# Five experts in place of four loaded ahead of the routing, with 64 places each, and the four large places sorted among the other eleven

## The chip, the cores and the metric

The kernel runs on one core of one Trainium2 chip, as one launch. The metric is the time on the device in microseconds (us), the median of the runs. Engines are named PE (TensorE), DVE (VectorE), ACT (ScalarE), POOL (GpSimd) and SP (SyncE, which issues nearly all loads of weights).

## What is computed

A trunk of four layers on 384 tokens (128 of context, 256 latents) of width 1024. Each layer is a token mixer followed by a mixture of 16 experts, of which each token takes two. Cut to the part that matters here:

```python
def moe(h, w_router, router_bias, w_gate, w_up, w_down):
    s = jax.nn.sigmoid((h @ w_router).astype(jnp.float32))
    ...
    _, idx = lax.top_k(jnp.where(emask, sb, -jnp.inf), TOP_K)      # TOP_K = 2, one group of four experts
    ...
    a = jnp.einsum('bsd,edf->bsef', h, w_gate)       # 16 experts, 1024 x 256 each
    u = jnp.einsum('bsd,edf->bsef', h, w_up)         # 1024 x 256
    act = jax.nn.silu(a) * u * gates[..., None].astype(h.dtype)
    return jnp.einsum('bsef,efd->bsd', act, w_down)  # 256 x 1024
```

With float32 weights each of an expert's three matrices is 1 MB, so a layer's experts are 48 loads of 1 MB.

## The kernel before

**Places.** The kernel computes an expert only for the tokens that chose it. 384 tokens with two experts each are 768 rows; they are sorted into 1152 places. Four experts, the first `FIXED = 4`, have 64 places each whatever the router says. The other 12 are sorted by load in each layer: the four with the most rows get 96 places, the other eight 64. Which expert stands at which of these 12 positions is known only on the chip, when the router has run; its number is written into the small array `held`. In what follows expert e means position e in this order, and Ge, Ue and De are the loads of its gate, up and down matrices.

**Blocks.** The 1152 places are 9 blocks of 128, each of four tiles of 32 rows. A block is computed on PE by a gate-up of 64 matmuls (32 rows against 512 columns each), 8 transposes, and the down projection of 32 matmuls, which is issued one block late: gate-up(b), transposes, down(b−1), gate-up(b+1). A tile belongs to one expert, and before the change the experts of the blocks' tiles are

```
block 0: 0 0 1 1    block 3: 5 5 6 6    block 6: 10 10 11 11
block 1: 2 2 3 3    block 4: 6 7 7 7    block 7: 12 12 13 13
block 2: 4 4 4 5    block 5: 8 8 9 9    block 8: 14 14 15 15
```

More rows than places for an expert go to further steps of their own, which are run only if there are such rows.

**Weights.** SP issues the loads one after the other into 15 slots of 1 MB: 0 to 7 are the `ring`, 8 and 9 lie in `V`, 10 to 12 in `work`, 13 and 14 in `gbc`. A load waits on the semaphore `slot_used` of its slot, which the last user of the slot's earlier contents increments, and SP issues nothing past a load that waits. The order of the loads and the slot of each are planned when the kernel is built, by `plan_ring`: it has an estimated begin and end for the use of each load, takes among the next 16 the one that can start soonest, and charges 2.45 us for a load or 2.9 us for one of an expert from `FIXED` on. `homes` says which slots a load may go to, `opens` from when.

Loads of the experts below `FIXED` have a fixed address and can be issued during the mixer. A load of another expert reads its number from `held` (L763), after SP has waited once per layer for `held_ready` (the sort is done) and for `near_issued` (POOL has issued the gathers of the tokens' rows).

Of the kernel before, what the change touches and what calls it, by code (L numbers as in the profile page):

```python
# [25 lines left out]
UC = 256  # L26
R = 8
TILE = 32
FIXED = 4
WIDE, NARROW = 3 * TILE, 2 * TILE  # L30
LARGE = 4
SIZES = [NARROW] * FIXED + [WIDE] * LARGE + [NARROW] * (E - FIXED - LARGE)
STARTS = [sum(SIZES[:i]) for i in range(E)]
# [106 lines left out]
def last_block(i):  # L140

    return (STARTS[i] + SIZES[i] - 1) // P
# [65 lines left out]
def phase_of(key):  # L208

    name, L = key[0], key[1]  # L210
    if name[:3] == "moe":
        return L, "moe"
    return (L - 1, "route") if name == "mod" and key[2] < 2 and L > 0 else (L, "main")


def homes(key):

    name, (L, phase) = key[0], phase_of(key)
    if name in ("moe_g", "moe_u"):
        pairs = ((0, 1), (2, 3), (8, 9), (10, 11)) + (((4, 5),) if key[2] >= FIXED else ())  # L220
        return [pair if name == "moe_g" else pair[1:] for pair in pairs]
    if name == "moe_d":
        late = (13,) if last_block(key[2]) < BLOCKS - 3 else tuple(range(6)) + (8, 9, 10, 11) if key[2] >= E - FIXED else ()
        return [(slot,) for slot in (6, 7, 12) + late]
    if name == "wo":
        return [(slot,) for slot in (4, 5, 6, 7)]
    if phase == "route":
        return [(2,), (3,), (12,)] if key[2] == 0 and key[3] < 3 else [(slot,) for slot in (4, 5, 6, 7, 13)]
    if name == "ukv":
        return [(slot,) for slot in (0, 1, 2, 3)]  # L230
    if name == "mod" and key[2] < 2:
        return [(slot,) for slot in range(R)]
    return [(slot,) for slot in tuple(range(R)) + ((9, 13, 14) if KINDS[L] < 2 else (13, 14))]
# [15 lines left out]
def plan_ring():  # L249
# [5 lines left out]
    def opens(key):  # L255
        name, phase = key[0], phase_of(key)
        if name[:3] == "moe" and key[2] >= FIXED:
            return mark["held", phase[0]]
        return 0.0

    def choice(key):
        if key[0] == "moe_u":
            return None
        phase = phase_of(key)
        free = {home: max(max(free_at[s], home_opens(s, phase, mark)) for s in home) for home in homes(key)}
        best = min(free, key=free.get)
        at = max(free[best], opens(key))
        safe = [k for k in waiting if k != key and not (key[0] == "moe_g" and k == ("moe_u",) + key[1:])]
        return (at, best) if not safe or at <= min(begin[k] for k in safe) else None
# [8 lines left out]
    while waiting:  # L278
# [5 lines left out]
        at, _, key, home = min(found)  # L284
        span = LOAD_SPAN_MOE if key[0][:3] == "moe" and key[2] >= FIXED else LOAD_SPAN
        now = at + span * len(home)
# [53 lines left out]
def build(nc, A):  # L340
# [4 lines left out]
    with ctx:  # L345
        def sb(name, shape):
            return ctx.enter_context(nc.sbuf_tensor(name, shape, F32))
# [47 lines left out]
        move_of = sb("move_of", [P, E])  # L395
        place_key = sb("place_key", [P, E - FIXED])
        place_of = sb("place_of", [P, E - FIXED])
# [2000 lines left out]
```

## Time and profile before

| | |
|---|---|
| median of 3 runs | 1530.26 us (1529.27 to 1533.38) |
| the profiled execution, its time and its span | 1539.47 us, 1537.7 us |
| PE busy | 1399.2 us, 91% of the span |
| DVE, ACT, POOL busy | 624.9, 346.7, 233.2 us |
| SP's DMA queue (q1) | 95686 packets, 346.13 MB, 59.6% of the 16 DMA engines' time |
| all DMA | 412.96 MB, mean 269 GB/s |

The rows of the profile have start and length in us. `issue` in a chain is time in which the engine waited for nothing that the profile shows by name; PE's waits for the landing of weights are among it. All matmuls of the experts are issued by one helper, so that they have one line, L1867, and they are told apart by their number (64 for a gate-up, 32 for a down, 96 where both follow without a break) and by their place in the stage. The four expert stages lie at about 265 to 376, 606 to 730, 1025 to 1147 and 1389 to 1510 us.

### The profile page before, as it was taken

How to read it: one execution, taken by the hardware profiler on the slowest of the kernel's cores; microseconds unless marked ns; L12 is line 12 of the kernel's file. 1: busy time of each engine (PE TensorE's matmuls, PEld its weight loads, DVE VectorE, ACT ScalarE, POOL GpSimd, SP SyncE). 2: the span in 40 equal slices, each digit the busy share in tenths (PEclk: the TensorE clock that was granted, in tenths of full speed). 3: DMA queues.
4: the chain of work that ended last, by engine and by line, in shares of the span. 5: the costliest groups of instructions: out<-in, count | busy, mean ns of one | idle time of the engine just before them, and what ended most of it. 6: DMA issues, size and time to landing. Idle time of an engine off the chain costs nothing.

```text
span 1537.7 us, 25812 instructions
## 1 busy us (share of the span) xinstructions
PE 1399.2 (91%) x10352; PEld 844.3 (55%) x10352; DVE 624.9 (41%) x1450; ACT 346.7 (23%) x933; POOL 233.2 (15%) x295
## 2 busy tenths in 40 slices
PE   4999998998998998898989999988989999969985
PEld 1876685332776686333664456853327766854332
DVE  0136625433456525242522343254334247252435
ACT  1105512110214612110210343121102036121101
POOL 0100022111122022110200000221112000212103
PEclk9999999999999999999989999999999999979998
DMA  9998138999978238999857502489999880238994
GB/s 332 331 313 278 73 107 325 386 420 414 331 284 238 83 131 295 386 416 420 321 212 248 118 29 96 162 328 381 420 414 340 286 307 2 82 124 299 421 422 166
DMA packets 121633, 412.96 MB, mean 269 GB/s; under 512 B 13531, under 2 KB 55486, under 8 KB 96934
## 3 DMA queue, kind: packets, MB, share of 16 engines
q1 hardware_dynamic: 95686, 346.13, 59.6%
q0 software_dynamic: 18880, 61.23, 12.2%
q10 hardware_dynamic: 6944, 3.91, 0.8%
q8 instruction: 85, 1.39, 0.4%
q14 instruction: 38, 0.31, 0.1%
HBM read 387.12 MB, written 26.66 MB: 269 GB/s over the span
## 4 chain that ended last, share of the span: by engine, by line
PE 73%; DMA 8%; DVE 8%; issue 4%; ACT 3%; POOL 1%; SPq 1%; DVEq 0%; POOLq 0%; ACTq 0%
PE bank L1867 65%; PE bank L2037 3%; ACT pp L1165 2%; PE bank L2202 2%; DMA y_slots<-kT 2%; DMA V<-in_swa_wqkv 1%; DMA ids<-own_id,row_of 1%; DVE x L1297 1%; DMA hT<-h_rows,id_of 1%; PE bank L1922 1%; DMA xn<-y_slots,row_of 1%; DMA id_of<-ids 1%; DVE hT L1289 1%; SPq L689 1%; PE bank L2214 1%
## 5 line engine op out<-in xcount | busy, mean ns | idle before, releaser
L1867 PE MATMUL bank<-ring,pp 128*32 128x512 f32 x2112 | 342.9, 606 | 17.4 <-issue 13.4
L1867 PE MATMUL bank<-ring,hT 128*128 128x256 f32 (+3 forms) x998 | 233.3, 392 | 5.3 <-DVE hT L1289 2.7
L1867 PEld LDWEIGHTS bank<-ring,hT 128*128 128x128 f32 x998 | 181.3, 191 | 54.2 <-issue 26.8
L1867 PE MATMUL bank<-work,pp 128*32 128x512 f32 x704 | 176.1, 609 | 8.6 <-DVE kT L1735 5.1
L1867 PEld LDWEIGHTS bank<-ring,pp 128*32 128x32 f32 x2112 | 92.5, 111 | 157.5 <-issue 155.7
L1867 PE MATMUL bank<-ring,xn 128*128 128x256 f32 x768 | 168.2, 380 | 0.0
L1867 PEld LDWEIGHTS bank<-ring,xn 128*128 128x128 f32 x768 | 145.0, 190 | 19.4
L1867 PE MATMUL bank<-V,pp 128*32 128x512 f32 x480 | 114.0, 629 | 5.3 <-issue 4.7
L1165 ACT ACTIVATE pp<-bank,neg_max 128x384 f32<-128x384 f32 x192 | 96.7, 525 | 13.3 <-DVE neg_max L1631 10.1
L1743 DVE TENSOR_TENSOR pp<-bank,pp 128x256 f32<-128x256 f32 x36 | 15.3, 425 | 198.0 <-ACT pp L1235 198.0
L910 POOL TENSOR_TENSOR x<-x,pp 128x256 f32<-128x256 f32 x48 | 38.3, 799 | 371.0 <-DVE pp L1704 371.0
L1735 DVE TENSOR_TENSOR kT<-bank,xn 128x512 f32<-128x512 f32 x72 | 46.4, 687 | 113.6 <-PE bank L1867 107.6
L1867 PE MATMUL bank<-ring,condT 128*32 128x256 f32 x1120 | 77.6, 418 | 8.5 <-DMA ring<-in_w_mod 8.5
L1867 PE MATMUL bank<-kT,work 64*128 64x384 f32 (+3 forms) x384 | 81.1, 456 | 4.7 <-ACT work L1153 2.5
L1631 DVE TENSOR_REDUCE neg_max<-bank 128x1 f32<-128x384 f32 x192 | 79.0, 460 | 14.2 <-PE bank L1867 14.2
L1867 PEld LDWEIGHTS bank<-work,pp 128*32 128x32 f32 x704 | 44.2, 112 | 67.6 <-issue 67.1
L2037 PE MATMUL bank<-ident,pp 128*128 128x128 f32 x448 | 70.7, 284 | 11.6 <-ACT pp L1165 7.5
L1704 DVE TENSOR_TENSOR pp<-bank,gbc 128x256 f32<-128x256 f32 x48 | 20.4, 425 | 137.8 <-PE bank L1867 137.8
L1278 DVE COPY work<-bank 128x256 f32<-128x256 f32 (+1 forms) x27 | 13.9, 514 | 143.5 <-PE bank L1867 143.5
L1235 ACT ACTIVATE pp<-bank 128x256 f32<-128x256 f32 x36 | 13.8, 385 | 243.6 <-PE bank L1867 243.6
L2037 PEld LDWEIGHTS bank<-ident,pp 128*128 128x128 f32 x448 | 48.1, 142 | 36.9 <-ACT pp L1165 17.4
L1867 PEld LDWEIGHTS bank<-ring,condT 128*32 128x32 f32 x1120 | 36.9, 119 | 44.4 <-DMA ring<-in_w_mod 13.4
(279 smaller groups left out, 1793.3 us busy)
## 6 DMA issues: line engine op xcount, KB each, us to landing
ring<-in_w_mod SPq DMA_DIRECT2D x70, 1024.0 KB, 8.2
ring<-in_moe_w_gate SPq DMA_DIRECT2D x40, 1024.0 KB
ring<-in_moe_w_up SPq DMA_DIRECT2D x40, 1024.0 KB, 15.6
ring<-in_moe_w_down SPq DMA_DIRECT2D x36, 1024.0 KB
gbc<-in_w_mod SPq DMA_DIRECT2D x17, 1024.0 KB, 11.8
work<-in_moe_w_down SPq DMA_DIRECT2D x16, 1024.0 KB, 15.2
y_slots<-kT POOLq DMA_DIRECT2D x28, 512.0 KB, 8.6
work<-in_moe_w_gate SPq DMA_DIRECT2D x12, 1024.0 KB
```

The costliest lines, as they stand in the source:

```text
L689: sp.dma_start(dst.rearrange("p (k n) -> p k n", k=shape), src).then_inc(slot_full[slot], 16)
L910: nc.gpsimd.tensor_tensor(xs, xs, wo_tmp[:, g % 4, :], ALU.add).then_inc(x_mixed, 1)
L1165: ins = nc.scalar.activation(pp[:, 0, odd, at:at + w], job_bank(("S", L, j, half, odd))[:, c0:c0 + w], ACT.Exp, bias=neg_max[:, h, b:b + 1 ...
L1289: ins = V_.tensor_scalar(hT[:, k, b * P:(b + 1) * P], job_bank(key)[:, k * P:(k + 1) * P], amul[:, s, k, c:c + 1], modc[:, 2 * s, k, c:c + ...
L1297: link(V_.scalar_tensor_tensor(out=x[:, b, :], in0=rows[b], scalar=wk_early[:, k, b:b + 1], in1=x[:, b, :], op0=ALU.mult, op1=ALU.add))
L1631: last = V_.tensor_reduce(neg_max[:, h, b:b + 1], job_bank(key)[:, c0:c0 + w], AX.X, ALU.max, negate=True)
L1704: V_.tensor_tensor(wo_tmp[:, g % 4, :], job_bank(key)[:, 0:UC], gbc[:, 0, COND[b], u * UC:(u + 1) * UC], ALU.mult).then_inc(wo_mul, 1)
L1735: V_.tensor_tensor(ys[:, blk % 2, cols], bank[4 + half][:, :], slot_gate[:, cols], ALU.mult).then_inc(evacuated, 1)
L1867: return pe.matmul(out, lhsT, rhs, start=start, stop=stop)
L1922: ins = pe.transpose(job_bank(key)[:, k * P:(k + 1) * P], scaled[n % 2][b][:, at:at + P], ident[:, :])
L2037: ins = pe.transpose(bank[4 + odd][:, t * P:(t + 1) * P], pp[:, 0, odd, 512 * half + t * P:512 * half + (t + 1) * P], ident[:, :])
L2202: ins = pe.transpose(bank[6 + k // 4][:, k % 4 * P:(k % 4 + 1) * P], xg[:, slot, k * P:(k + 1) * P], ident[:, :])
```

## The change

`FIXED` becomes 5, so that five experts have fixed numbers and 64 places, and the four large places are sorted among the other eleven. The number of places, 1152, and of blocks, 9, stays.

```diff
@@ -26,7 +26,7 @@
-FIXED = 4
+FIXED = 5
 WIDE, NARROW = 3 * TILE, 2 * TILE
 LARGE = 4
 SIZES = [NARROW] * FIXED + [WIDE] * LARGE + [NARROW] * (E - FIXED - LARGE)
@@ -217,7 +217,7 @@
     name, (L, phase) = key[0], phase_of(key)
     if name in ("moe_g", "moe_u"):
-        pairs = ((0, 1), (2, 3), (8, 9), (10, 11)) + (((4, 5),) if key[2] >= FIXED else ())
+        pairs = ((0, 1), (2, 3), (8, 9), (10, 11)) + (((4, 5),) if key[2] >= FIXED - 1 else ())
```

What hangs on `FIXED`: the experts of blocks 2 to 4 become 4 4 5 5, 5 6 6 6 and 7 7 7 8 (the other blocks stay); `held` and the arrays of the sort have 11 entries in place of 12; G4, U4 and D4 have a fixed address and no wait for `held_ready`; and `plan_ring` gives another order and other slots. The second line lets G4 and U4 still use slots 4 and 5.

The order on SP, early in the first layer's expert stage (G is `in_moe_w_gate`, U is `in_moe_w_up`, D is `in_moe_w_down`; this piece begins with D0). Before:

```order
L689 DMA work<-in_moe_w_down 128x2048 [waits slot_used12,states,o_ready]
L689 DMA ring<-in_moe_w_down 128x2048 [waits slot_used6]
L689 DMA ring<-in_moe_w_down 128x2048 [waits slot_used7]
L689 DMA gbc<-in_moe_w_down 128x2048 [waits slot_used13,wo_mul]
L763 TENSOR_LOAD held [waits near_issued,held_ready]
L763 ISA x2
L689 ISA [waits slot_used4]
L689 DMA ring<-in_moe_w_gate 128x2048
L689 DMA ring<-in_moe_w_up 128x2048 [waits slot_used5]
```

After, at the same place:

```order
L689 DMA work<-in_moe_w_down 128x2048 [waits slot_used12,states,o_ready]
L689 DMA ring<-in_moe_w_down 128x2048 [waits slot_used6]
L689 DMA ring<-in_moe_w_gate 128x2048 [waits slot_used4]
L689 DMA ring<-in_moe_w_up 128x2048 [waits slot_used5]
L689 DMA ring<-in_moe_w_down 128x2048 [waits slot_used7]
L689 DMA gbc<-in_moe_w_down 128x2048 [waits slot_used13,wo_mul]
L763 TENSOR_LOAD held [waits near_issued,held_ready]
L763 ISA x2
L689 ISA [waits slot_used0]
L689 DMA ring<-in_moe_w_gate 128x2048
```

G4 and U4 have moved ahead of D2, D3 and the wait for `held_ready`; the first load behind the wait is G5, into slot 0. (In the fourth layer they stand between D2 and D3.)

The second place is the end of the same stage on SP. Before, the piece goes from D10 to D12:

```order
L689 DMA ring<-in_moe_w_down 128x2048 [waits slot_used7]
L763 TENSOR_LOAD held
L763 ISA x2
L689 ISA [waits slot_used4]
L689 DMA ring<-in_moe_w_gate 128x2048
L689 DMA ring<-in_moe_w_up 128x2048 [waits slot_used5]
L689 DMA ring<-in_moe_w_down 128x2048 [waits slot_used6]
L763 TENSOR_LOAD held
L763 ISA x2
L689 ISA [waits slot_used0]
L689 DMA ring<-in_moe_w_gate 128x2048
L689 DMA ring<-in_moe_w_up 128x2048 [waits slot_used1]
```

After, from D10 to U15:

```order
L689 DMA work<-in_moe_w_down 128x2048 [waits slot_used12]
L689 DMA ring<-in_moe_w_down 128x2048 [waits slot_used4]
L763 TENSOR_LOAD held
L763 ISA x2
L689 ISA [waits slot_used0]
L689 DMA ring<-in_moe_w_gate 128x2048
L689 DMA ring<-in_moe_w_up 128x2048 [waits slot_used1]
L763 TENSOR_LOAD held
L763 ISA x2
L689 ISA [waits slot_used10]
L689 DMA work<-in_moe_w_gate 128x2048
L689 DMA work<-in_moe_w_up 128x2048 [waits slot_used11]
```

The order was D10, G14, U14, D11, G15, U15, and is D10, D11, G14, U14, G15, U15. In all layers the loads ahead of U15 are the same ones. The order of the instructions of PE, ACT, POOL and DVE does not move; DVE's operations of the sort are 11 and 121 elements wide in place of 12 and 144.

## Rows read from the trace of the kernel before

**Rows 1.** The page: busy us, share of the span, instructions of PE and others

```profile
PE 1399.2 (91%) x10352; PEld 844.3 (55%) x10352; DVE 624.9 (41%) x1450; ACT 346.7 (23%) x933; POOL 233.2 (15%) x295
```

**Rows 2.** Windows: stretch, us, busy PE to POOL, granted clock, DMA share, GB/s

```profile
602.00:611.40 9.40, 7.69 (x70) 7.45 (x66) 7.29 (x32) 0.96 (x2) 3.03 (x3) 1.00 1.03 350
628.00:702.00 74.00, 70.72 (x611) 24.87 (x607) 27.46 (x45) 8.83 (x20) 12.52 (x13) 0.98 1.01 414
...
284.00:374.00 90.00, 83.13 (x725) 29.45 (x728) 33.65 (x54) 9.59 (x22) 12.34 (x13) 0.98 1.02 420
...
1044.00:1144.00 100.00, 92.10 (x789) 31.91 (x785) 34.67 (x56) 10.56 (x24) 13.57 (x15) 0.97 1.00 413
...
1361.00:1387.80 26.80, 16.16 (x105) 15.25 (x106) 17.54 (x82) 4.29 (x8) 3.99 (x5) 0.62 0.16 60
1397.00:1402.00 5.00, 2.91 (x20) 1.26 (x22) 3.04 (x6) 2.52 (x4) 0.24 (x1) 0.81 0.90 54
```

**Rows 3.** Timeline of SP's loads: start, us; second layer, then fourth layer

```profile
602.21 0.33 SPq L689 DMA_DIRECT2D gbc<-in_moe_w_down  x1
611.39 0.17 SPq L689 DMA_DIRECT2D ring<-in_moe_w_gate  x1
...
702.42 0.37 SPq L689 DMA_DIRECT2D ring<-in_moe_w_up  x1
...
1356.15 0.33 SPq L689 DMA_DIRECT2D gbc<-in_moe_w_down  x1
1387.87 0.17 SPq L689 DMA_DIRECT2D ring<-in_moe_w_gate  x1
...
1396.93 0.33 SPq L689 DMA_DIRECT2D ring<-in_moe_w_gate  x1
...
1409.65 0.34 SPq L689 DMA_DIRECT2D V<-in_moe_w_gate  x1
```

**Rows 4.** The chain late in the four stages: start, us, what

```profile
346.88 2.60 issue
349.49 8.41 PE bank L1867 x64
...
358.93 1.47 issue
360.39 3.67 PE bank L1867 x32
...
701.74 7.07 PE bank L1867 x64
...
709.84 3.12 issue
712.96 5.37 PE bank L1867 x32
...
1127.21 2.80 issue
...
1475.67 2.76 issue
1478.43 8.77 PE bank L1867 x64
...
1494.54 10.54 PE bank L1867 x96
```

**Rows 5.** PE's timeline where gate-up(8) starts, in the first three layers

```profile
365.57 8.79 PE L1867 MATMUL bank<-ring,pp 128*32 128x512 f32 x80 [1.10 <-issue]
...
718.66 10.51 PE L1867 MATMUL bank<-ring,pp 128*32 128x512 f32 x96
...
1135.71 10.51 PE L1867 MATMUL bank<-ring,pp 128*32 128x512 f32 x96
```

**Rows 6.** DMA issues from 702.0 to 704.5 us: KB, us to landing

```profile
ring<-in_moe_w_up SPq DMA_DIRECT2D x1, 1024.0 KB, 15.4
```

**Rows 7.** Window of gate-up(7) in the first layer, columns as in rows 2

```profile
349.40:358.90 9.50, 9.41 (x72) 3.28 (x72) 1.09 (x4) 0.39 (x1) 0.00 (x0) 0.85 1.01 423
```

## The prediction

> **What bounds the kernel now.** I began with the busy times: PE works 1399.2 us of the 1537.7 us span [rows 1], so only its waits can give anything, and a later view has to say what ends them in the expert stages. The windows by stretch come second. In the second layer's stage (L1) the DMA engines are busy all the time: a share of 1.03 from 602.0 to 611.4 us, 1.01 from 628 to 702 us at 414 GB/s [rows 2]. A load is 1,048,576 bytes, so it costs 1.048576/414 = 2.53 us of that stream. The first and the third layer look the same, 1.02 and 1.00 over 90 and 100 us [rows 2]. The reader is to see here that the stream of weights has no hole in those three layers. The fourth (L3) has one: a share of 0.16 from 1361 to 1387.8 us [rows 2].
>
> Third comes SP's timeline, which tells when loads are issued. In L1 SP issues D3 (into `gbc`) at 602.21 and then nothing until G4 at 611.39 [rows 3], because it waits for `held_ready` and `near_issued`. Over just those 9.2 us the DMA share is 1.03 [rows 2]: the queue is still emptying what stands in it. SP's pause costs no byte. In L3, D3 goes out at 1356.15 and G4 at 1387.87 [rows 3], and there the share of 0.16 shows the queue empty.
>
> Fourth, the chain of waits, with the names of the blocks put to it by counting (a block is a gate-up of 64 matmuls, 8 transposes, then the down projection of the block before, 32 matmuls). PE waits late in each stage. L1: gate-up(7) takes 7.07 us from 701.74; at 709.84 PE waits 3.12 us for D11, then down(6) takes 5.37 us; gate-up(8) follows at 718.66 [rows 4, 5]. L0: 2.60 us before gate-up(7), 1.47 before down(6). L2: 2.80 before down(6). L3: 2.76 before gate-up(7) [rows 4].
>
> **What pins gate-up(8).** U15, the last load that it needs, is issued at 702.42 in L1 and lands 15.4 us later [rows 3, 6]: 717.82 us, and gate-up(8) starts at 718.66. So block 8 starts when U15 has landed, whatever PE did before.
>
> **The change, part by part.**
>
> *Early move, L0 to L2: 0 us.* G4 and U4 no longer read the register of a held expert, so they go ahead of D2 and D3 and of SP's wait. In a queue without a hole that only swaps places: 2.53 × 2 = 5.1 us earlier for two loads, 5.1 us later for D2 and D3, and U15 behind the same number of bytes. The first load behind the wait is now G5, and D3 leaves the queue two loads later, so the queue is if anything fuller there. D2 and D3 are first used by down(1), some 20 us on, so their delay costs nothing; without that cover it would cost up to 5.1 us in each layer. If the queue did run dry, the gain could reach those 5.1 us; the share of 1.03 excludes it.
>
> *Early move, L3: −1.4 us.* Here G4 and U4 really fill a hole. But G5 waits for slot 0, which block 0's gate-up gives back, and is issued at 1396.93 now [rows 3] and still is. From 1397 to 1402 the queue hardly moves, 54 GB/s [rows 2], so the four loads G5, U5, G6, U6 end at about 1402 + 4 × 2.53 = 1412.1 us. G7 waits for block 1's slot and is issued at 1409.65 [rows 3]. The stream can't get ahead of that: the gain lies between 0 and 1412.1 − 1409.65 = 2.5 us. An issued load needs some time before its bytes move; I take 1.4, about the middle.
>
> *Late move: D11 ahead of G14 and U14, into slot 4.* D11 now lands two loads (5.1 us) earlier. It was waited for 1.47 to 3.12 us, so the wait before down(6) goes in all four layers. U15 has the same loads ahead of it, so its landing stays. Its slots (10 and 11 in place of 0 and 1) must be free in time: the landing lag of 15.4 us is six loads of queue, and a slot given back some us later would still find bytes ahead. What PE gains before down(6) it therefore waits before gate-up(8). Worked out:
> - L0: gate-up(7) and its transposes end at 358.93, down(6) takes 3.57 without a fall of the clock, the turns 0.5: ready at 363.0. Gate-up(8) starts at 365.57 [rows 4, 5]. New wait 2.6, start as before.
> - L1: 709.84 + 4.1 = 713.9, landing 717.8: wait 3.9 to 4.2. The start moves from 718.66 to about 718.15 (down(6) with its slow clock had ended a little after the landing): −0.5.
> - L2: 1127.21 + 4.1 = 1131.3 against a start at 1135.71 [rows 4, 5]: wait 3.9, also −0.5.
> - L3: the wait of 2.76 shrinks to 1.4 and gate-up(7) then takes 7.07 in place of 8.77 [rows 4]; ready at 1475.67 + 1.4 + 7.07 + 1.02 + 4.0 = 1489.2; the landing moves from before 1494.54 to before 1493.1: wait 3.9, −1.4.
>
> *The clock after the new wait.* After 2.60 us without work gate-up(7) took 8.41 us in place of 7.07, after 2.76 it took 8.77; after 3.12 down(6) took 5.37 in place of about 3.6; after 1.47 down(6) took 3.67 [rows 4]. The granted clock of gate-up(7) in L0 is 0.85 on average [rows 7], so part of it ran at 1.2 GHz in place of 2.4. A long wait thus costs 1.3 to 1.8 us more. In L1 and L2 that price is paid now on down(6), where it lies in front of U15's landing and costs nearly nothing. In the changed kernel it falls on gate-up(8), and behind that nothing waits for a load that is late anyway: it is on the path. I take +1.3 for L0 (the same 2.60 us), +1.75 each for L1 and L2, +1.7 for L3. Bounds: 0 each, and 1.8 each.
>
> The Trainium skill, page "TensorE: Matmul & The Clock Gate", section "HAM oscillation — how this bites in real kernels", describes a kernel whose waits for DMA between short stretches of matmuls send the clock down each time. This case's trace agrees, with 8.77 for 7.07 us after a 2.76 us wait; by the page as by the rows the longer wait before block 8 speaks against the change.
>
> *Everything else: 0.* DVE's sorting operations get 11 wide where they were 12; they take about 0.3 us each and are fixed cost mostly. One register fewer is read per layer while the queue is deep. Expert 8's weights are needed one block earlier (block 4 holds a part of it); the order gives them some 4 us of slack in L0, my count of places in the queue, and more elsewhere. With that slack gone, each layer would lose what is missing. The work of PE is the same 9 blocks.
>
> **Sum.** L0 +1.3; L1 −0.5 + 1.75 = +1.25; L2 +1.25; L3 −1.4 + 1.7 = +0.3. Together +4.1, of which I let some 0.4 go for what a narrower sort and a better filled queue may give: +3.7. The profiled execution took 1539.47 us with its span of 1537.7, so 1543.2 for such a one; the median of the runs shown is 1530.26, 9.2 below, and the difference is carried over: **1534.0 us**.
>
> **The rivals.**
> 1. *The two early loads are a gain in every layer.* SP's pause ends sooner for PE: 5.1 us in each of four layers, 1530.3 − 20 = 1510 us. For it speaks only the pause of 9.2 us in SP's timeline; against it the share of 1.03 in it. Chance 0.05. The Trainium skill, page "DMA: Bandwidth & Descriptors", section "Rules for kernel authors", says to issue a load early and to wait for it late; by that rule this is what the change would do. The trace speaks against it in three layers of four.
> 2. *No fall of the clock is added and L3 gains more,* by gathers that run while the queue is empty: −2.4 without the clock's price, and another −2.5 to −4 in L3: about 1525 us. Chance 0.07.
> 3. *Slower: the merged wait costs its full price.* Place: gate-up(8) of all layers. 4 × 1.8 − 1.0, and no gain in L3 because the stall at 1397 to 1402 swallows it: +6.2, 1536.5 us. It decides once the price is over 1.9 us a layer, or L3's gain stays away. For it: the new waits (3.9 us) are longer than any in the rows. Chance 0.24. If the low clock lasted twice as long as it does after 2.8 us, it were 4 × 3.5 − 2.4 = +11.6, 1542 us. Chance 0.06.
> 4. *Expert 4 gets more than 64 rows* where it had 96, and the overflow steps run: 3 passes × 16 experts with 3 loads of 2.53 us each is 364 us more for one such layer, about 1895 us. Before there were none and I count at most 59 rows for expert 4 in these inputs. Chance 0.02.
> 5. *The forecast,* merged waits with part of their price given back: 0.56.
>
> **How the numbers follow.** A measurement of this kernel can tell about 0.3%, 4.6 us, from no change. Same is the forecast's 0.56. Faster is 0.05 + 0.07 = 0.12; slower 0.24 + 0.06 + 0.02 = 0.32. The range goes from no price at all (−2.4, 1527.9) and a bit of case 2 up to case 3 with its run-to-run share of 2 us: 1527 to 1539. Outside it are case 1, most of case 2, the doubled fall and the overflow, 0.2 in all.
>
> **What would show it.** Right: D11 no longer waited for in any layer; one wait of 2.6 to 4.2 us before gate-up(8), starting within 0.5 us of today's place (L3: 1.4 earlier) as counted from the stage's start; gate-up(8) at 8.4 to 8.8 us; the DMA share still at 1.00 from the router to D15 in L0 to L2. Wrong: U15's landing earlier by two loads in L0 to L2 (case 1); U15 late because its slots 10 and 11 come free late; a wait before gate-up(4) or down(4) for expert 8; gate-up(8) at 7.07 us.

## The result

The changed kernel takes 1541.24 us (median of 20 runs, 1533.13 to 1550.74), the kernel before, run beside it, 1534.16 us (20 runs, 1529.02 to 1540.01). The ratio is 1.0046, interval 1.003 to 1.0062: slower by 7.1 us of 1534. The forecast was 3.7 us slower, "same" the likeliest and "slower" at 0.32. The direction was right. The time of 1541.24 lies outside the range of 1527 to 1539. Of the 7.2 us between the forecast of 1534.0 and this time, 3.9 come from its base: it started from the 1530.26 of three runs, and twenty runs of the same kernel give 1534.16. The other 3.4 were missing in the sum. One run of warm (5014.88 us) and one of late_alone (1845.43 us), two of the experiments below, were slow and stand in no ratio.

The two profiled executions, 1539.47 us before and 1541.63 after, lie only 2.2 us apart. That hides 4.6 us: between the third and the fourth expert stage the profiled execution of before took 237.9 us (end of down(8) at 1151.57 to gate-up(0) at 1389.47), that of after 233.3 us (1155.56 to 1388.81), and those of the nine executions of the experiments below 233.1 to 235.8. So the stages are compared by themselves, from the start of gate-up(0) to the end of down(8):

| us, from PE's timeline | L0 | L1 | L2 | L3 | sum |
|---|---|---|---|---|---|
| stage, before | 121.40 | 122.75 | 122.80 | 120.91 | 487.86 |
| stage, after | 121.41 | 125.49 | 123.98 | 123.84 | 494.72 |
| start of gate-up(8), after − before | +0.01 | +0.10 | −1.59 | −1.76 | −3.24 |
| from there to the start of down(8), before | 12.21 | 12.21 | 12.22 | 12.20 | |
| the same, after | 12.21 | 14.85 | 14.99 | 15.19 | +8.40 |
| down(8), after − before | 0 | 0 | 0 | +1.70 | +1.70 |

The stages are 6.9 us longer, close to the measured 7.1. The closeness is partly luck, for these are single executions: two of one and the same kernel (late_undone, below) differ by 4.0 us in this sum. The stretch from gate-up(8) to down(8) is steadier: in the four executions with D11 behind U14 it takes 12.20 to 12.29 us in all 16 layers. In these two profiles all of the loss lies behind the start of gate-up(8).

### The profile page after: what moved, and what is told of

The parts are those of the page before. It is cut to its first block, busy times and chain, and to the rows that moved or that the text cites. A ratio compares the mean times of both kernels' runs of the same rounds, so it can differ in the third digit from the quotient of the medians.

```text
span 1539.8 us, 25784 instructions
## 1 busy us (share of the span) xinstructions
PE 1396.0 (91%) x10352; PEld 842.3 (55%) x10352; DVE 624.5 (41%) x1450; ACT 346.7 (23%) x933; POOL 233.6 (15%) x295
## 3 DMA queue, kind: packets, MB, share of 16 engines
q0 software_dynamic: 18880, 61.07, 12.2%
## 4 chain that ended last, share of the span: by engine, by line
PE 70%; DMA 11%; DVE 7%; issue 5%; ACT 3%; POOL 2%; SPq 1%; another core or an unknown queue 0%; POOLq 0%; DVEq 0%; ACTq 0%
PE bank L1867 62%; PE bank L2037 3%; ACT pp L1165 2%; DMA hT<-h_rows,id_of 2%; PE bank L2202 1%; DMA V<-in_swa_wqkv 1%; DMA ids<-own_id,row_of 1%; DMA id_of<-ids 1%; DMA ring<-in_moe_w_gate 1%; DMA work<-in_moe_w_gate 1%; DMA y_slots<-kT 1%; PE bank L1922 1%; DMA xn<-y_slots,row_of 1%; POOL ids L924 1%; SPq L689 1%
## 5 line engine op out<-in xcount | busy, mean ns | idle before, releaser
L1867 PE MATMUL bank<-ring,pp 128*32 128x512 f32 x2064 | 375.0, 608 | 31.3 <-issue 19.2
L1867 PEld LDWEIGHTS bank<-ring,pp 128*32 128x32 f32 x2064 | 99.7, 112 | 190.0 <-issue 188.1
L1867 PE MATMUL bank<-V,pp 128*32 128x512 f32 x496 | 117.2, 627 | 2.7 <-issue 2.2
## 6 DMA issues: line engine op xcount, KB each, us to landing
ring<-in_moe_w_gate SPq DMA_DIRECT2D x37, 1024.0 KB, 12.5
gbc<-in_w_mod SPq DMA_DIRECT2D x17, 1024.0 KB, 11.6
```

What stands on the lines that cost most here:

```text
L1867: return pe.matmul(out, lhsT, rhs, start=start, stop=stop)
```

## The profile after

The page of the changed kernel, busy times and the queue that SP feeds:

```profile
PE 1396.0 (91%) x10352; PEld 842.3 (55%) x10352; DVE 624.5 (41%) x1450; ACT 346.7 (23%) x933; POOL 233.6 (15%) x295
q1 hardware_dynamic: 95686, 346.13, 59.4%
```

PE does the same 10352 instructions as in [rows 1] and the queue carries the same bytes. Busy times tell nothing here. SP's timeline in L1 (start, us, what), first the early place, then the tail:

```profile
595.21 0.33 SPq L689 DMA_DIRECT2D work<-in_moe_w_down  x1
596.06 0.33 SPq L689 DMA_DIRECT2D ring<-in_moe_w_down  x1
598.88 0.33 SPq L689 DMA_DIRECT2D ring<-in_moe_w_gate  x1
600.61 0.33 SPq L689 DMA_DIRECT2D ring<-in_moe_w_up  x1
600.98 0.47 SPq L689 DMA_DIRECT2D ring<-in_moe_w_down  x1
601.56 0.47 SPq L689 DMA_DIRECT2D gbc<-in_moe_w_down  x1
618.47 0.35 SPq L689 DMA_DIRECT2D ring<-in_moe_w_gate  x1
...
684.64 0.38 SPq L689 DMA_DIRECT2D ring<-in_moe_w_down  x1
695.46 0.34 SPq L689 DMA_DIRECT2D ring<-in_moe_w_gate  x1
```

G4 went out at 598.88, 12.5 us earlier than in [rows 3], and SP then issued nothing for 16.9 us (601.56 to 618.47), since G5 waits for block 0's slot. The windows (columns as in [rows 2]) say that the queue was never dry in these stretches of L1, and that in L3 it was:

```profile
601.60:618.40 16.80, 14.88 (x132) 10.00 (x133) 7.07 (x31) 0.92 (x2) 7.72 (x8) 1.00 1.02 374
628.00:702.00 74.00, 68.35 (x591) 24.04 (x587) 28.37 (x46) 8.84 (x20) 12.69 (x14) 0.98 1.01 417
1361.00:1396.00 35.00, 22.81 (x178) 17.14 (x177) 18.57 (x84) 4.87 (x9) 10.11 (x11) 0.76 0.31 110
```

A pause of SP nearly twice as long as before's still costs no byte: the share is 1.02 within it. Now the chain at the end of the stage in L1 (start, us, what), which answers to the rows from 701.74 of [rows 4]:

```profile
715.23 2.83 issue
718.06 13.19 PE bank L1867 x96
```

The wait of 3.12 us ahead of down(6) is gone, and one of 4.01 us is ahead of gate-up(8), where PE's timeline shows it (the number in brackets is the idle time), beside a wait of 1.53 us ahead of gate-up(7) that cost nothing:

```profile
701.94 0.62 PE L1867 MATMUL bank<-ring,pp 128*32 128x512 f32 x2 [1.53 <-issue]
...
718.06 1.07 PE L1867 MATMUL bank<-ring,pp 128*32 128x512 f32 x2 [4.01 <-issue]
```

A pair of matmuls takes 0.62 us behind the wait of 1.53, and 1.07 behind the wait of 4.01. The windows of two us show why, in the last but two column, the granted clock:

```profile
709.00:714.00 5.00, 5.00 (x44) 2.05 (x42) 1.20 (x3) 0.97 (x2) 0.00 (x0) 1.00 1.04 428
714.00:716.00 2.00, 0.04 (x1) 0.00 (x0) 1.89 (x3) 0.37 (x1) 0.29 (x1) 1.00 0.96 397
716.00:718.00 2.00, 0.00 (x0) 0.00 (x0) 1.32 (x2) 0.00 (x0) 0.24 (x1) 0.65 1.01 422
718.00:720.00 2.00, 1.94 (x12) 0.68 (x16) 0.00 (x0) 0.00 (x0) 0.00 (x0) 0.50 1.01 420
720.00:722.00 2.00, 2.00 (x12) 0.45 (x8) 0.00 (x0) 0.00 (x0) 0.00 (x0) 0.50 1.00 420
722.00:724.00 2.00, 2.00 (x16) 0.59 (x12) 0.00 (x0) 0.00 (x0) 0.00 (x0) 0.64 1.02 426
724.00:726.00 2.00, 2.00 (x24) 0.67 (x20) 0.00 (x0) 0.00 (x0) 1.17 (x2) 1.00 1.04 434
```

The clock falls to 0.50, which is 1.2 in place of 2.4 GHz, within the wait and is still there in 718 to 722 us and for most of 722 to 724 (0.64), with 12 matmul records in two us where there are 24 at full clock. By these windows that is some 5.4 us of gate-up(8) at half clock (an estimate), which makes the 2.64 us that it takes longer. In L3 the chain has the fall twice:

```profile
1489.34 2.79 issue
1492.12 8.43 PE bank L1867 x64
...
1505.87 1.30 DVE kT L1735 x2
1507.17 0.14 issue
1507.31 5.37 PE bank L1867 x32
```

Gate-up(8) takes 8.43 for 7.07 us, and down(8), which is short of work before it, 5.37 for about 3.6. Here the rows of matmuls alone would mislead: the 96 matmuls from 1492.12 read 11.83 us, but DVE's next step comes only at 1505.87, 13.75 us after their start. That is why the table counts from start to start. ACT's next step is late too, 1.83 us behind the start of the last transposes (0.54 in the kernel before, L1), though the granted clock reads 1.00 (two windows, then two rows of the timeline):

```profile
1496.00:1498.00 2.00, 2.00 (x24) 0.67 (x20) 0.00 (x0) 0.00 (x0) 0.00 (x0) 1.00 0.98 404
1504.00:1506.00 2.00, 0.39 (x2) 0.20 (x2) 0.13 (x1) 0.29 (x1) 0.82 (x1) 1.00 0.82 287
...
1503.88 0.51 PE L2214 MATMUL bank<-ident,pp 128*128 128x128 f32 x2
1505.71 0.37 ACT L669 COPY pp<-bank 128x256 f32<-128x256 f32 x1 [4.41 <-PE bank L2214]
```

Both engines wait for PE here. So of the 8.40 us in the table, 5.4 are gate-up(8)'s own matmuls (9.71, 8.50 and 8.39 us in L1 to L3 for 7.07). The other 3.0 come in L2 and L3 behind them, where PE waits 2.62 and 2.92 us ahead of down(8) in place of 1.27, at a granted clock of 1.00. That PE really finished later than its records say is the likely reading; what held it up is not shown.

In L0 the wait ahead of gate-up(7) was 2.64 us, gate-up(7) took 10.03 us in place of 8.41, and PE came late enough to gate-up(8) that only 1.02 us of wait was left, with no fall (10.51 us). There the clock's price was paid ahead of U15's landing, and L0 lost nothing.

## The experiments

All ratios are to the kernel before, timed beside each. "Stages" is the sum of the four stages as in the table, of the profiled execution, against 487.86 before. "Block 8" is what the four stretches from the start of gate-up(8) to down(8) take over 4 × 12.2 us. The code pieces are shortened to the lines that matter.

| | ratio (interval) | stages | block 8 |
|---|---|---|---|
| the change | 1.0046 (1.003 to 1.0062) | +6.9 | 8.4 |
| old_plan | 0.9982 (0.9964 to 1.0001) | −0.2 | 0 |
| new_plan | 1.0144 (1.0123 to 1.0165) | +24.3 | 6.4 |
| late_undone | 0.9981 (0.9961 to 1.0001) | +0.9 | 0.1 |
| late_undone_2 | 0.9989 (0.9972 to 1.0006) | +4.9 | 0 |
| early_undone | 1.003 (1.0013 to 1.0048) | +7.0 | 4.5 |
| late_alone | 1.0049 (1.0024 to 1.0073) | +9.2 | 10.7 |
| warm | 1.0064 (1.0044 to 1.0084) | +10.4 | 0.9 |
| warm_short | 1.0009 (0.9991 to 1.0027) | +3.7 | 1.4 |
| warm_half | 1.003 (1.001 to 1.0049) | +10.4 | 4.4 |

**1. old_plan: the change without its order of loads**

```diff
-    ring_place, ring_order = plan_ring()
+    ring_place, ring_order = planned(4)     # plan_ring() under FIXED = 4 and the STARTS that go with it
```

> The changed kernel in all (five fixed experts, places, sort of eleven), but its loads in the order and slots of the kernel before: D2, D3, then G4, U4 and D11 behind U14. My theory, that the cost sits in D11 ahead of G14 and U14 and the one long wait that it makes before gate-up(8): a ratio to the kernel before of 1.000 (0.998 to 1.002), gate-up(8) with down(7) at 10.5 us in L1 to L3. Rival, that the new mix of experts in the blocks or the narrower sort costs it: 1.004 to 1.005, as the changed kernel.

Measured: 0.9982, waits of before's kind (in L1 2.04 us ahead of gate-up(7), 1.14 ahead of down(6), 1.11 ahead of gate-up(8)), and 12.2 us from gate-up(8) to down(8) in all four layers. So 64 places for expert 4, the new mix of experts in blocks 2 to 4 and the sort of eleven cost nothing. The order of loads does. One part of the early move stays in this run: G4 and U4 stand behind D3, but have no wait for `held_ready`, and in L1 G4 goes out at 601.72 us, where it was 611.39.

**2. new_plan: the order and slots of the change on the kernel before**

```diff
+    ring_place, ring_order = planned(5)
+    for L in range(DEPTH):        # G4 and U4 stay behind D3
+        ring_order = behind(ring_order, [("moe_g", L, 4), ("moe_u", L, 4)], ("moe_d", L, 3))
```

> The kernel before in all (four fixed experts), but its loads in the order and slots of the changed one, only G4 and U4 kept behind D3 and the wait for held_ready. My theory: a ratio of 1.004 to 1.006, a wait of about 4 us before gate-up(8) in L1 to L3 and 12 to 13 us for gate-up(8) with down(7). Rival, that the early move or the places cost it: 1.000.

Measured: 1.0144, more than any theory gave. The timeline of SP and a window in its L1 show what I had overlooked:

```profile
677.07 0.34 SPq L689 DMA_DIRECT2D work<-in_moe_w_gate  x1
677.51 0.38 SPq L689 DMA_DIRECT2D work<-in_moe_w_up  x1
693.94 0.33 SPq L689 DMA_DIRECT2D ring<-in_moe_w_down  x1
...
690.00:702.00 12.00, 12.00 (x109) 4.05 (x108) 4.34 (x6) 1.41 (x5) 2.23 (x2) 1.00 0.73 259
```

The changed plan puts G11 into slot 10 behind G6 and, next after U11, D9 into slot 7 behind D6. In the changed kernel expert 6 ends in block 3, in the kernel before in block 4, one block of 12 us later. So D9 goes out 16.4 us after U11 (677.51 to 693.94), where it is 9.0 us in the changed kernel (666.43 to 675.38). SP issues in order, so all loads behind D9 wait too; the queue falls behind (share 0.73 from 690 to 702 us) and gate-up(7) waits 7.14 us. This run tests the late move only together with this hole, so it is no evidence for my theory. It shows that a plan belongs to its places.

**3. late_undone: the change with D11 back behind U14**

```diff
     for L in range(DEPTH):
+        order = behind(order, [("moe_d", L, 11)], ("moe_u", L, 14))
```

> The changed kernel with one pair swapped back in each layer: D11 issued behind U14, slots as in the changed kernel, G4 and U4 early. My theory: the wait splits again into one before down(6) and none or a short one before gate-up(8), the fall of the clock lies in front of U15's landing, ratio to the kernel before 0.998 to 1.001. Rival, that slots 10, 11 or the early move are to blame: 1.004 to 1.005.

Measured: 0.9981. The chain in L1:

```profile
711.85 3.26 issue
715.11 3.67 PE bank L1867 x32
```

PE's timeline has 1.11 us idle ahead of gate-up(8), and 12.20 us from its start to down(8), in L1 as in the other layers. One position in the order, that of D11, makes the whole difference between 1.0046 and 0.998: about 0.6%, 9 to 10 us by the two runs of this kernel, against 8.4 + 1.7 in the table of stages. The changed plan also moves D8 ahead of G10 and U10 and gives other slots, which the section on the change leaves out; late_undone keeps both, so they are not what costs.

**4. early_undone: the change with only its early move undone**

```diff
+        order = behind(order, [("moe_g", L, 4), ("moe_u", L, 4)], ("moe_d", L, 3))
...
-                if (L, FIXED) not in held_at and e >= FIXED:
+                if (L, FIXED) not in held_at and e >= FIXED - 1:
```

(the second edit stands ahead of the direct load, so that G4 waits for `held_ready` as before)

> The changed kernel with only its early move undone: G4 and U4 issued behind D3 and behind the wait for held_ready and near_issued, the tail (D11 ahead of G14 and U14) as in the changed kernel. My theory, that the early move gives nothing in L0 to L2 and 1.4 to 1.8 us in L3: a ratio to the kernel before of 1.004 to 1.007, U15 at its place in L0 to L2 and some 1.5 us later in L3. Rival, that G4 and U4 ahead of D2 and D3 do harm (to the gathers, or by D2 and D3 late): 1.000 to 1.002.

Measured: 1.003, below the expected 1.004 to 1.007 and above the rival's 1.000 to 1.002. From gate-up(8) to down(8) it took 14.44 us in L1 and L3, behind waits of 3.99 and 2.44 us, and 12.20 in L0 and L2. In L0 the wait was 2.28 us, without a fall; in L2 a slow gate-up(7) of 9.97 us had left only 1.09 us of it. In L3 gate-up(8) starts 104.77 us into the stage, 103.31 in the change and 105.07 before. The ratios (1.003 and 1.0046) overlap. The cost remains without the early move.

**5. late_alone: the kernel before with only the late move**

```diff
+        new.update({("moe_d", L, 11): 4, ("moe_g", L, 14): 0, ("moe_u", L, 14): 1, ("moe_g", L, 15): 2,
+                    ("moe_u", L, 15): 3, ("moe_d", L, 12): 5, ("moe_d", L, 13): 6})
+        order = behind(order, [("moe_d", L, 11)], ("moe_d", L, 10))
```

> The kernel before with only the late move: D11 issued right behind D10 and ahead of G14 and U14. So that it needs no slot that comes free late, D11 goes to slot 4, G14 and U14 to 0 and 1, G15 and U15 to 2 and 3, D12 and D13 to 5 and 6. My theory: a ratio of 1.004 to 1.007, one wait of about 4 us before gate-up(8) and 12 to 13.2 us for gate-up(8) with down(7) in most layers. Rival, that the late move costs only together with the new places or the early loads: 0.999 to 1.001.

Measured: 1.0049. Its chain in L1:

```profile
717.70 2.78 issue
720.49 13.61 PE bank L1867 x96
...
735.76 1.45 PE bank L1867 x9
```

The waits ahead of gate-up(8) are 4.00, 4.32, 4.33 and 2.31 us in L0 to L3, and from its start to down(8) it takes 15.30, 15.27, 14.89 and 14.04 us against 12.2. This is what new_plan was meant to be: the late move alone, on the kernel before, with slots that come free in time, costs as much as the change.

**6. warm, warm_short, warm_half: the order of the change, with work for PE in the wait**

```diff
+                    pe.wait_ge(act_full, n + 1)
+                    for _ in range(WARM.get((L, blk), 0)):
+                        mm(bank[slot][:, 0:P], ident[:, :], ident[:, :], True, True)
                     for e in sorted(set(of)):
                         wait_unit(("moe_g", L, e))
```

> The changed kernel, order of loads untouched, with added matmuls of ident by ident on PE (128 columns each, about 0.13 us by the transposes' rate) into the bank that gate-up(8) overwrites, before it waits for its weights: 28 ahead of gate-up(8) in each layer, 14 ahead of gate-up(7) in L0 and L3. My theory, that the price is the low clock after the wait: gate-up(8) with down(7) at 10.5 us in all layers, starting where it starts now; L3's 5.3 us for down(8) back at 3.6; together 6 to 9 us off the changed kernel, a ratio to the kernel before of 0.999 (0.997 to 1.001). Rival, that the loads of down(7) or something else stretch block 8: no change from 1.0046, or more by the work that is added.

Measured: 1.0064. A matmul of float32 leaves two records here, and 28 of them take 6.42 us, not 3.6 (28 × 0.13). PE's timeline in L1:

```profile
721.01 6.42 PE L1867 MATMUL bank<-ident 128*128 128x128 f32 x56
727.36 0.62 PE L1867 MATMUL bank<-ring,pp 128*32 128x512 f32 x2
```

Gate-up(8) with down(7) is back at 10.51 us in all layers (12.21 to 12.62 to down(8)), and L3's down(8) at 3.64, as my theory has it. But the added work overran the wait: gate-up(8) starts 110.23 us into the stage in L1, where it was 107.00. The forecast of the ratio was wrong by my count of the matmuls' length. So, again, with 17:

> The changed kernel with fewer added matmuls of ident by ident than in the run before, since 28 of them took 6.4 us (0.23 us each) and overran the wait: 17 (3.9 us) ahead of gate-up(8) in each layer, 10 and 9 ahead of gate-up(7) in L0 and L3. My theory: gate-up(8) with down(7) at 10.5 us, starting when U15 has landed, within 0.5 us of the changed kernel: a ratio of 0.998 to 1.001. Rival, that the low clock is not what costs: 1.004 to 1.006.

Measured: 1.0009 (0.9991 to 1.0027). PE's timeline in L1:

```profile
715.71 3.96 PE L1867 MATMUL bank<-ident 128*128 128x128 f32 x34
720.04 0.62 PE L1867 MATMUL bank<-ring,pp 128*32 128x512 f32 x2 [0.37 <-issue]
```

Same order of loads, more work, and less time: gate-up(8) starts at 107.42 us into the stage in L1 (107.00 in the change) and runs at 10.51 us in all four layers. To down(8) it takes 12.50, 12.20, 12.20 and 13.27 us, 1.4 over in place of 8.4, and down(8) of L3 takes 3.64. Some 5.7 of the 7.1 us come back by the ratios (1.0046 − 1.0009, of 1534). What costs is that PE stands idle in the wait, and the low clock that follows, not the late start as such. In L3 1.1 us remain, without any fall of the clock in the profile.

> The changed kernel with half the added matmuls: 8 (1.85 us) ahead of gate-up(8) in each layer, 5 ahead of gate-up(7) in L0 and L3, so that some 2.1 us of the wait before gate-up(8) stay without work. My theory, with waits of 1.0 to 2.2 us ahead of full speed in the traces so far and 2.3 us and more ahead of slow blocks: gate-up(8) with down(7) at 10.5 us in at least two of L1 to L3, a ratio of 0.999 to 1.003. Rival, that any wait there costs its fall: 1.004 to 1.006.

Measured: 1.003. Half the work does not do: with 2.14 to 2.18 us of wait left, block 8 took 14.43 us to down(8) in L0, 14.10 in L1 (and down(8) 6.36 us there) and 12.43 in L3. By its letter my expectation held (10.51 in three layers, and 1.003 at the edge of its range), but it counted only the matmul records: in L1 they read full speed while the next step comes 1.9 us late. It also took over 2.3 us as the length of wait that brings a fall. Old_plan's 2.04 us ahead of gate-up(7) had been followed by 8.77 us already, and here 2.17 us were followed by 8.77 for gate-up(8) in L0.

**7. late_undone once more**

> The same kernel as late_undone, a second time, to see whether it is faster than the kernel before (0.9981, 0.9961 to 1.0001 the first time). My theory: the early move and the new places are worth 0 to 1.8 us, so 0.9985 to 1.000. Rival, that they are worth the 2.9 us measured first: 0.998.

Measured: 0.9989 (0.9972 to 1.0006); with the first run some 0.15% below the kernel before, with 1 inside both intervals. It is no version that I would call faster. In this execution the waits ahead of down(6) in L2 and L3 (2.95 and 2.64 us) were followed by 6.58 and 5.34 us for down(6), and gate-up(8) and down(7) still took 10.51 us, 12.2 to down(8).

## Why the prediction fell short

- **What bounds the stage** (the stream of weights, and U15's landing the start of gate-up(8)): right. The share stays at 1.00 to 1.02 where SP pauses, and all loss lies behind that landing.
- **The base:** 1530.26 from three runs was 3.9 us under the 1534.16 of twenty, and this alone carried the measured time out of the range: moved by 3.9 us the range would end at 1543. That the time falls beside the 1542 of the doubled fall in rival 3 is chance, for that one meant 11.6 us more than before.
- **Early move, 0 in L0 to L2 and −1.4 in L3:** right in kind. In L3 gate-up(8) began 1.76 us earlier, but single executions of one kernel differ by 1.15 there (late_undone's two). The six in which G4 goes out early and no added work overruns the wait start it at 103.3 to 104.8 us into the stage, the three without (new_plan and its hole aside) at 104.8 to 105.1: 1.0 us on average.
- **Late move, the wait merges ahead of gate-up(8):** right in place and size: 4.01, 3.96 and 3.98 us against the forecast 3.9 to 4.2 in L1, 3.9 in L2 and L3. The forecast that L1 would start gate-up(8) 0.5 us earlier did not come (+0.10). In L0 it was 1.02 in place of 2.6, because gate-up(7) had its slow clock for 10.03 us.
- **The clock after the new wait: the step that failed, by its size.** I took 1.3 + 1.75 + 1.75 + 1.7 = 6.5 us and put 1.8 a layer as the bound. Measured from the start of gate-up(8) to down(8): 0, 2.64, 2.77 and 2.99, together 8.4, over the bound in three layers. The price in the sum was only how much longer the matmuls of the slowed block took. For that part I had 5.2 us in L1 to L3, and it measured 5.4, though unevenly (2.64, 1.43, 1.32). What the sum lacked are the 3.0 us that come behind gate-up(8) in L2 and L3, before down(8). L0's 1.3 did not come.
- **Why the price was higher** is only in part shown. My first reading was the length of the wait: the prices came from waits of 2.6 to 3.1 us, the new ones were 4 us. Behind the wait of 3.12 us in [rows 4] the clock is still full when work resumes at 712.96 and falls afterwards, as the first three windows below show; behind 4 us in the change's L1 it has fallen already. But in late_alone's L1 it was still full behind 4.32 us, when work resumed at 720.49 (last two windows), and the block cost 3.07 us all the same. Shorter waits ahead of gate-up(8) could cost nearly as much: 2.90 us brought 2.7 (new_plan, L2), 2.44 brought 2.2 (early_undone, L3). I saw that the waits would be longer than any in the rows and put this on rival 3 (0.24) without raising the price.

```profile
712.00:714.00 2.00, 1.04 (x12) 0.50 (x16) 0.00 (x0) 0.00 (x0) 0.00 (x0) 1.00 1.04 426
714.00:716.00 2.00, 2.00 (x15) 0.54 (x8) 0.00 (x0) 0.00 (x0) 0.00 (x0) 0.51 0.97 406
716.00:718.00 2.00, 2.00 (x16) 0.54 (x8) 0.00 (x0) 0.00 (x0) 0.00 (x0) 0.63 1.04 434
...
717.00:720.50 3.50, 0.01 (x3) 0.04 (x4) 2.34 (x3) 0.00 (x0) 0.53 (x1) 1.00 1.00 417
720.50:724.00 3.50, 3.50 (x20) 1.11 (x24) 0.00 (x0) 0.00 (x0) 0.00 (x0) 0.60 1.02 425
```

- **What I had no term for:** down(8) of L3 at 5.34 us, +1.7, seen too in early_undone (5.31). It stands behind the slowed block, with PE idle for 2.92 us before it (1.80 in early_undone). Late_alone's L1 had 2.64 us idle there and 3.64 for down(8). That the one fall brings the other is only argued.
- **The 0.4 us let go** for a better filled queue: L2 and L3 together started gate-up(8) 3.35 us earlier, where I had 1.9. Single profiles of one kernel differ by as much there (late_undone's two executions: 107.86 and 108.93 in L2), so this is not settled.
- **How the parts add up:** against the +3.7 of the sum, L0's price −1.3, gate-up(8)'s matmuls +0.2, the time before down(8) +3.0, down(8) of L3 +1.7, the earlier starts −0.8 and the 0.4 let go back again: +6.9, the profiled stages.
- **Rivals:** 1 (two loads gained in each layer) fell: gate-up(8) of L0 and L1 starts where it did, and late_undone with the early move is at 0.998. By the rule of the Trainium skill, page "DMA: Bandwidth & Descriptors", section "Rules for kernel authors", to issue a load early, nothing came in L0 to L2, as the trace of before had said: with the share at 1.02 while SP pauses, an earlier issue was only another place in the same line. Rival 3, the full price, is what happened, at a higher price than it had and with L3's gain. No overflow ran: PE has the same 10352 instructions.

## What to carry to other kernels

When loads bound a stage and PE waits for them in several short pieces, an order of loads that gathers these pieces into one wait can cost time though no byte comes later. Ask where the wait stands: ahead of the last load's landing the low clock cost nothing here, behind it it was paid. Price a fall of the clock from the start of the block to the start of the next dependent step, since that came up to 1.9 us later than the matmuls' own records said. And take the base of a forecast from as many runs as the result will have.

A slot of a ring is only as free as the last block that uses it. A plan made for one layout of experts, run on another, cost 1.4%, with slots that came back a block later and an engine that issues its loads in order.

## What I had not expected of the hardware

- The same wait did not always bring a fall. Ahead of down(6), 3.26 us (late_undone, L1) and 3.23 us (L2) were followed by 3.64 us, full speed, while 3.12 and 2.80 in the kernel before were followed by 5.34, and 2.64 (late_undone_2, L3) by 5.34. All seven waits of 3.96 us and more ahead of gate-up(8) (three each in the change and in late_alone, one in early_undone) were followed by a slow block. The nine waits of 2.14 to 2.90 us there, in four kernels, brought anything from nothing to 2.7 us.
- Down(8) started up to 1.9 us late behind blocks that show full speed and a full clock (warm_half, L1: 1.9 us; warm_short, L3: 1.1), only in kernels with D11 ahead of G14. The cause stays open.
- Work of no use made the kernel faster: 17 matmuls that fill a 4 us wait took it from 1.0046 to 1.0009, while 8, which left 2.1 us, gave 1.003.
- A plain float32 matmul of 128 columns took 0.23 us (6.42 us for 28), where I had 0.13 by the rate of the transposes.
- The changed kernel's 20 runs span 17.6 us, those of before 11.0. That the merged wait does this is not shown: early_undone has it too, and its 12 runs span 8.7.
